# A hybrid two-layer model on one core: state-space chunks spread over two heads, a shared phasor table, and the rotation of the scanned states on GpSimd

## What is computed

```python
proj = hn @ w_in                       # 512 state-space inputs u, then q, k, v, g of 6 retention heads of 256
# state space: 32 groups of 16 channels, 64 complex states each = 16 columns of 128 states
dt = exp(log_dt); mag = exp(lam_re * dt); th = lam_im * dt
ab = mag * (cos(th) + i sin(th)); f = (ab - 1) / lam     # discretisation
bu = u @ (f * b)
x[t] = ab * x[t-1] + bu[t]             # associative scan over the 256 tokens
y = gelu(Re(c x) + d u); y_s5 = y * sigmoid(y @ glu_w + glu_b)
# retention: per head rope(q), rope(k), (q k^T * decay) v, rms norm, times silu(g)
h = h + concat(y_s5, y_ret) @ w_out    # then a gated conv feed-forward, then an attention layer and another one
```

## Time and profile before

| | |
|---|---|
| median of 3 runs | 2261.57 us (2256.18 to 2261.68) |
| profiled execution | 2257.0 us, its span 2255.2 us |
| PE (TensorE matmul) busy | 2162.7 us, 96% |
| DVE (VectorE) busy | 1471.7 us, 65% |
| ACT (ScalarE) busy | 1003.2 us, 44% |
| POOL (GpSimd) busy | 776.3 us, 34% |

### The profile page before, as it was taken

How to read it: one execution, slowest core, us unless ns; L and a number is a source line. 1 busy time by engine, 2 the same in 40 slices (tenths; PEclk the granted TensorE clock), 3 DMA queues, 4 the chain that set the end, 5 groups by cost and what they waited for, 6 DMA issues and landing times.

```text
span 2255.2 us, 47390 instructions
## 1 busy us (share of the span) xinstructions
PE 2162.7 (96%) x18426; PEld 2132.9 (95%) x18426; DVE 1471.7 (65%) x1747; ACT 1003.2 (44%) x1244; POOL 776.3 (34%) x880
## 2 busy tenths in 40 slices
PE   8788888999999999999999999999999999999997
PEld 8788777999999999999999989999999999999997
DVE  6378766577666655666666666677666555666666
ACT  4243333444444444444444445545444444444442
POOL 5799995023434300433411000023443101443311
PEclk9899998999999999999999999999999999999999
DMA  6334233454555456555455533455554556554553
GB/s 262 114 135 154 98 135 125 158 201 178 207 200 187 166 193 221 196 194 186 176 187 198 192 125 123 162 192 188 206 187 174 186 193 220 197 187 185 174 197 114
DMA packets 64604, 398.69 MB, mean 177 GB/s; under 512 B 7169, under 2 KB 9729, under 8 KB 29057
## 3 DMA queue, kind: packets, MB, share of 16 engines
q1 hardware_dynamic: 60192, 391.15, 48.2%
q10 hardware_dynamic: 4320, 6.27, 0.8%
HBM read 395.29 MB, written 2.10 MB: 176 GB/s over the span
## 4 chain that ended last, share of the span: by engine, by line
PE 81%; POOLq 9%; POOL 5%; issue 2%; DVE 2%; ACT 1%; DVEq 0%; DMA 0%; ACTq 0%
PE PS L1401 25%; PE PS L1402 25%; PE PS L1405 25%; POOLq L1288 2%; POOLq L1292 2%; POOL g L1290 2%; POOL E L1293 2%; POOLq L1159 2%; POOLq L1166 1%; PE PS L1396 1%; PE PS L1397 1%; PE PS L1398 1%; POOLq L1306 1%; POOL S L1305 1%; PE PS L1751 0%
## 5 line engine op out<-in xcount | busy, mean ns | idle before, releaser
L705 DVE TENSOR_TENSOR lo<-raw,hi 128x1024 fp32r<-128x1024 f32 (+2 forms) x826 | 950.4, 1170 | 527.0 <-ACT hi L356 521.8
L356 ACT ACTIVATE hi<-raw 128x1024 fp32r<-128x1024 f32 (+2 forms) x826 | 785.8, 969 | 722.2 <-PE PS L1405 676.1
L1401 PE MATMUL PS<-XS,hi 128*128 128x256 f32 x3584 | 851.6, 280 | 8.2 <-ACT hi L356 8.2
L1402 PE MATMUL PS<-XS,hi 128*128 128x256 f32 x3584 | 845.4, 278 | 0.0
L1401 PEld LDWEIGHTS PS<-XS,hi 128*128 128x128 f32 x3584 | 680.2, 190 | 15.8 <-issue 15.4
L1402 PEld LDWEIGHTS PS<-XS,hi 128*128 128x128 f32 x3584 | 680.4, 190 | 0.4
L1405 PE MATMUL PS<-XS,lo 128*128 128x256 f32 x3584 | 480.8, 277 | 0.0
L1405 PEld LDWEIGHTS PS<-XS,lo 128*128 128x128 f32 x3584 | 441.5, 188 | 0.0
L1401 PE MATMUL PS<-YF,hi 128*128 128x256 f32 x1408 | 331.8, 276 | 0.0
L1402 PE MATMUL PS<-YF,hi 128*128 128x256 f32 x1408 | 331.8, 276 | 0.0
L1358 POOL TENSOR_TENSOR ctmp<-apad,cws 128x512 f32<-128x512 f32 x88 | 131.9, 1519 | 526.0 <-DVE apad L756 526.0
(11 more groups left out here) (238 smaller groups left out, 2487.7 us busy)
## 6 DMA issues: line engine op xcount, KB each, us to landing
raw<-in_ffn_up SPq DMA_DIRECT2D x176, 1024.0 KB, 4.8
raw<-in_ffn_dn SPq DMA_DIRECT2D x128, 704.0 KB, 4.1
raw<-in_w_in SPq DMA_DIRECT2D x51, 1024.0 KB, 4.9
raw<-in_w_oe SPq DMA_DIRECT2D x16, 1024.0 KB, 4.8
raw<-in_w_oo SPq DMA_DIRECT2D x16, 1024.0 KB, 4.8
raw<-in_mla_dn SPq DMA_DIRECT2D x9, 1024.0 KB, 4.8
raw<-in_w_ukv SPq DMA_DIRECT2D x8, 1024.0 KB, 4.8
raw<-in_w_uq SPq DMA_DIRECT2D x8, 768.0 KB, 4.3
```

What stands on the lines that cost most here:

```text
L356: act.activation(hi[:, p % SLOTS, 0:n], raw[:, u % SLOTS, off:off + n], ACT.Copy).then_inc(hi_ready, 1)
L705: V.tensor_tensor(lo[:, p % SLOTS, 0:n], raw[:, u % SLOTS, off:off + n], f(hi[:, p % SLOTS, 0:n]), ALU.subtract).then_inc(lo_ready, 1)
L1401: mm(PS[:, bank, 0:T], wh, x[:, 0:T], start=first, stop=False)
L1402: mm(PS[:, bank, 0:T], wh, x[:, T:2 * T], start=False, stop=False)
```

## The change

It has five parts. (1) The levels n = 1 to 16 of all 16 columns are made once (`first_phasors`, the table `E32` in the tile `sums`), and a chunk's `phasors` copies 32 phasors from it and does levels 5 to 7. (2) The rotation forwards moves from VectorE to GpSimd (`rotate_out`), behind a new semaphore `scanned`. (3) The work of a chunk is spread: its second scan comes behind the split of the next head's second K piece, its second C product behind the third K piece of the next head, its B products at other pieces. (4) The end of a head (scaling of G, norm, gate, low half) stands between the splits of the next head instead of behind its own. (5) The set-up is divided: GpSimd computes the exponentials and the powers, VectorE the sine, cosine, factor and B in four parts between the splits of head 0; the transposes of B stand behind the V pieces of head 0 instead of the third G piece; the last sums of squares come earlier, and the first two columns of `U` are scaled ahead of two splits.

GpSimd, and the programs of the chunk:

```diff
+            def double(e, n, lo_, cos_, sin_):
+
+                pool.drain()
+                c_, s_ = lo_
+                G.tensor_tensor(c_, e[:, :, :, 0:n], cos_, ALU.mult)
+                G.tensor_tensor(s_, e[:, :, :, 0:n], sin_, ALU.mult)
+                pool.drain()
+                G.tensor_tensor(e[:, 0, :, n:2 * n], c_[:, 0], s_[:, 1], ALU.subtract)
+                G.tensor_tensor(e[:, 1, :, n:2 * n], c_[:, 1], s_[:, 0], ALU.add)
...
+            def first_phasors():
+
+                G.memset(E32[:, 0, :, 0:1], 1.0)
+                G.memset(E32[:, 1, :, 0:1], 0.0)
+                for l in range(5):
+                    n = 1 << l
+                    c, s_ = (ph[:, l, ri, :].unsqueeze(1).unsqueeze(3).broadcast_to([P, 2, KD, n]) for ri in range(2))
+                    double(E32, n, (g1m[:, :, :, 0:n], g2m[:, :, :, 0:n]), c, s_)
+                pool.drain()
 
             def phasors(k, h0, r):
 
                 m = 4 * h0 + 2 * k
-                G.tensor_copy(phst[:, :, :, :], ph[:, :, :, m:m + 2] if r is None else ph[:, :, :, ds(r * 4 + m, 2)])
                 e = E[:, k]
-                G.memset(e[:, 0, :, 0:1], 1.0)
-                G.memset(e[:, 1, :, 0:1], 0.0)
-                for l in range(8):
+                pool.drain()
+                G.tensor_copy(phst[:, :, :, :], ph[:, 5:8, :, m:m + 2] if r is None else ph[:, 5:8, :, ds(r * 4 + m, 2)])
+                G.tensor_copy(e[:, :, :, 0:32], E32[:, :, m:m + 2, :] if r is None else E32[:, :, ds(r * 4 + m, 2), :])
+                for l in range(5, 8):
                     n = 1 << l
-                    pool.drain()
-                    c, s_ = (phst[:, l, ri, :].unsqueeze(1).unsqueeze(3).broadcast_to([P, 2, 2, n]) for ri in range(2))
-                    G.tensor_tensor(g1[:, :, :, 0:n], e[:, :, :, 0:n], c, ALU.mult)
-                    G.tensor_tensor(g2[:, :, :, 0:n], e[:, :, :, 0:n], s_, ALU.mult)
-                    pool.drain()
-                    G.tensor_tensor(e[:, 0, :, n:2 * n], g1[:, 0, :, 0:n], g2[:, 1, :, 0:n], ALU.subtract)
-                    G.tensor_tensor(e[:, 1, :, n:2 * n], g1[:, 1, :, 0:n], g2[:, 0, :, 0:n], ALU.add)
+                    c, s_ = (phst[:, l - 5, ri, :].unsqueeze(1).unsqueeze(3).broadcast_to([P, 2, 2, n]) for ri in range(2))
+                    double(e, n, (g1[:, :, :, 0:n], g2[:, :, :, 0:n]), c, s_)
...
+            def rotate_out(k, h0, r):
+
+                pool.wait_ge(scanned, at(2 * h0 + k + 1, 2, r))
+                e = E[:, k]
+                G.tensor_tensor(sT2, sT1, e[:, 0:1].broadcast_to([P, 2, 2, T]), ALU.mult)
+                G.tensor_tensor(sB, sT1, e[:, 1:2].broadcast_to([P, 2, 2, T]), ALU.mult)
+                pool.drain()
+                G.tensor_tensor(sT1[:, 0], sT2[:, 0], sB[:, 1], ALU.subtract)
+                G.tensor_tensor(sT1[:, 1], sT2[:, 1], sB[:, 0], ALU.add).then_inc(z_ready, 1)
...
+            def s5_chunk(h0, r):
+
+                if h0:
+                    stage(h0, r)
                 phasors(0, h0, r)
-                pool.drain()
+                rotate_in(0, h0, r)
                 pool.wait_ge(cst_in, at(16 * h0 + 16, 16, r))
                 G.tensor_tensor(Cst[:, :, 1, :], Cst[:, :, 1, :], minus[:, 0:1].unsqueeze(2).broadcast_to([P, 4, 32]),
                                 ALU.mult).then_inc(cneg_ready, 1)
-                rotate_in(0, h0, r)
                 phasors(1, h0, r)
+                rotate_out(0, h0, r)
                 rotate_in(1, h0, r)
+                rotate_out(1, h0, r)
 
             G.memset(minus[:, :], -1.0)
             pool.wait_ge(small_in, 16)
-            pool.wait_ge(den_ready, 1)
-            s5_setup()
+            s5_magnitude()
+            s5_powers()
             pool.wait_ge(bank_free, 2)
             pool.wait_ge(bt_ready, 2)
+            stage(0, None)
+            first_phasors()
             s5_chunk(0, None)
             with pool.Fori(0, 3) as r:
                 s5_chunk(1, r)
```

VectorE: the scans, the places of the head's end, and the set-up:

```diff
@@ -833,25 +946,38 @@
                     dve.wait_ge(w_ready, S_(k + 1, 2))
                     for ri in range(2):
                         for m in range(2):
-                            V.tensor_tensor_scan(sT1[:, ri, m, :], magst[:, m:m + 1].broadcast_to([P, T]),
-                                                 sB[:, ri, m, :], 0.0, ALU.mult, ALU.add)
-                    dve.drain()
-                    eb = E[:, k]
-                    V.tensor_tensor(sT2, sT1, eb[:, 0:1].broadcast_to([P, 2, 2, T]), ALU.mult)
-                    V.tensor_tensor(sB, sT1, eb[:, 1:2].broadcast_to([P, 2, 2, T]), ALU.mult)
-                    dve.drain()
-                    V.tensor_tensor(sT1[:, 0], sT2[:, 0], sB[:, 1], ALU.subtract)
-                    V.tensor_tensor(sT1[:, 1], sT2[:, 1], sB[:, 0], ALU.add).then_inc(z_ready, 1)
-
+                            ins = V.tensor_tensor_scan(sT1[:, ri, m, :], magst[:, m:m + 1].broadcast_to([P, T]),
+                                                       sB[:, ri, m, :], 0.0, ALU.mult, ALU.add)
+                    ins.then_inc(scanned, 1)
...
                 for i in range(4):
-                    if h0 == 0 or i:
-                        split(p0 + 4 + i, 16, r)
+                    if h0 and i == 0:
+                        gate_and_variance(r, h0 - 1)
+                    split(p0 + 4 + i, 16, r)
+                    if h0 == 0:
+                        (s5_angles, s5_phasor, s5_factor, s5_b)[i]()
+                    if h0 and i == 0:
+                        norm_head(r, h0 - 1)
+                    if h0 and i == 1:
+                        head_output(r, h0 - 1)
+                if h0 > 1:
+                    y5()
+                if h0:
+                    y_low(r, h0 - 1)
                 rotate(KRo, p0 + 4, e0)
 
                 for i in range(4):
                     split(p0 + 8 + i, 16, r)
-                    if s5 and i == 1:
+                    if s5 and i == 0:
                         scan(0)
...
-                if s5:
-                    scan(1)
                 if glu:
                     dve.wait_ge(glu_sig, 1)
                     V.tensor_tensor(sigs, sigs, U[:, :, :], ALU.mult).then_inc(glu_mul, 1)
 
                 for i in range(4):
                     split(p0 + 16 + i, 16, r)
+                    if s5 and i == 1:
+                        scan(1)
                     if glu and i == 1:
...
-                scale_banks(Gr[:, :, :], p0 + 16, e0 + 3, 16, r)
-                dve.wait_ge(osum_done, H_(1, 1))
-                norm_head(H_(1, 1))
-                if not glu:
-                    split(p0 + 20, 16, r)
+
+            def gate_and_variance(r, g):
+
+                scale_banks(Gr[:, :, :], 24 + 16 * g, 5 + 4 * g, 16, r)
+                dve.wait_ge(osum_done, at(g + 1, 1, r))
+                V.tensor_scalar(nwt[:, 0, :], PS[:, 4, 0:T], 1.0 / RD, EPS, ALU.mult, ALU.add).then_inc(ovar_ready, 1)
+
+            def norm_head(r, g):
+
+                dve.wait_ge(osd_ready, at(g + 1, 1, r))
+                newton(ro, sq[:, 0, :])
...
+            def s5_angles():
+
+                th, cs, sn, a, b, c = (col(i) for i in (2, 3, 4, 5, 6, 7))
+                dve.wait_ge(th_ready, 1)
...
@@ -801,8 +914,8 @@
                 if c == 0:
                     lambda_squared()
             root(0)
+            scale_banks(U[:, 0:2, :], 7, 0)
             splits(8, kinds=("std",) * 2)
-            scale_banks(U[:, 0:2, :], 7, 0)
             scale_banks(U[:, 2:4, :], 8, 1)
             splits(10, kinds=("std",) * 2)
             dve.wait_ge(even_loads, 48)
```

ScalarE, in `even_head`:

```diff
                 for i in range(4):
-                    if h0 == 0 or i:
-                        split(p0 + 4 + i, 16, r)
-                    if s5 and i == 1:
-                        bu_copy(0)
+                    split(p0 + 4 + i, 16, r)
+                    if h0 and i == 0:
+                        root_and_gate(r, h0 - 1)
+                    if s5 and i in (1, 2):
+                        bu_copy(i - 1)
+                    if s5 and i == 2:
+                        load_c()
+                    if glu and i == 2:
+                        act.wait_ge(c_done, 8)
+                        act.dma_start(gluw, A["gluw"]).then_inc(gluw_in, 16)
+                if h0:
+                    round_y(r, h0 - 1)
...
-                for i in range(4):
-                    split(p0 + 8 + i, 16, r)
-                    if s5 and i == 0:
-                        bu_copy(1)
-
+                splits(p0 + 8, 16, r)
                 for i in range(4):
                     split(p0 + 12 + i, 16, r)
-                    if s5 and i < 2:
-                        bu_copy(i + 2)
+                    if s5 and i in (1, 2):
+                        bu_copy(i + 1)
```

TensorE:

```diff
@@ -1462,11 +1560,9 @@
             for p in range(8):
                 if p % 2 == 0:
                     x_split(0)(p // 2)
-                if p == 6:
-                    x_squares(3)
                 std_piece(p, p // 2, pair(p % 2), XSk)
```

(102 more changed lines are left out.)

213 lines of the change are left out of this document (113 added, 100 removed).

## The result

| | before | changed |
|---|---|---|
| median of 4 runs of each | 2260.24 us (2256.18 to 2261.68) | 2282.83 us (2281.31 to 2285.02) |
| profiled execution, its span | 2257.0, 2255.2 us | 2285.02, 2283.2 us |
| granted clock, mean of the span | 0.982 | 0.975 |

The changed kernel is slower: ratio 1.0104, 95% interval 1.0086 to 1.0121, 22.6 us between the medians. Forecast were +15 and 2276, with a range to 2294.

The account below looks back on a forecast made before the run. GpSimd was taken to bound the heads at 68.4 us a turn; the change makes a ring of 43 + 33 = 76 us. 100.2+4P-378.2-11 gives +15: 2272 profiled, 2276 median, range 2250 to 2294.

Parts of the forecast that it names:

- The ring: Chunk loop: GpSimd's turn becomes a ring with hand-overs, two legs of 43 and 33 us, 76 us against 68.4 before.
- 4P-289: Time difference from before in us, P being one chunk-loop turn on GpSimd; P = 76 gives +15, break-even is 72.3.
- z1 to z0: From a chunk's second rotation out to the next chunk's first: all GpSimd, 32.4 us plus 10.6 of collisions, 43 us.
- z0 to z1: From a chunk's first rotation out to its second: chain through four engines, 33 us, with 18.3 of TensorE work.
- The end of the heads: Last chunk: its second C product, behind three K pieces of head 5, waits shortly without half clock; 11 us back.
- Head 0: First head: the 15.3 us wait goes, TensorE stalls 6 us at the first V piece, head 1 begins about 97.6.
- no relief: GpSimd's uncollided turn: table removes small steps, rotation out adds two blocks of 7.4 us; from 43 to about 47 us.
- VectorE loses 2 x 3.7 us and has slack anyway: Chunk loop: moving the rotation out to GpSimd takes 2 x 3.7 us off VectorE, which was not short of time.
- The ring's waits cost nothing: Rival: GpSimd stays the only bound, turn 68.4 us, time 2246; chance 0.19 together with the rival of vanishing collisions.
- Collisions mostly vanish: Rival: collisions go with the small steps, turn 62 to 66 us, 2221 to 2236; 0.19 shared with the no-cost-waits rival.
- An even swap: Rival: turn 70.6 to 74 us, time within 7 us of before; chance of landing within 0.17.
- VectorE too late in head 0: Rival: small set-up steps at 0.4 us when meeting GpSimd's powers add 7 us, 2283 with turn 76; no separate chance.

Follow-up runs that it names:

- kernel 1: The changed kernel with the rotation of the scanned states back on VectorE, everything else as changed; 2236.73 us, ratio to before 0.9909.
- kernel 4: The changed kernel with VectorE's splits in heads 1 to 4 cut to 64 of 1024 columns, same instruction count; 2238.49 us, ratio to before 0.9913.
- kernel 9: The changed kernel with the second scan ahead of the splits of the next head's K pieces; 2283.66 us, ratio to before 1.0108.
- kernel 6: The kernel before plus the shared phasor table and the divided set-up, rotation and chunk order as before; 2220.92 us, ratio to before 0.9837.
- kernel 2: The kernel before plus the shared phasor table alone; 2240.20 us, ratio to before 0.9917.
- kernel 8: kernel 6 with the rotation of the scanned states moved to GpSimd, in the order of before; 2273.08 us, ratio to before 1.0065.
- kernel 3: The kernel before with only the rotation of the scanned states moved to GpSimd; 2312.12 us, ratio to before 1.0238.
- kernel 7: kernel 1 with the first scan and its rotation behind the second split of the V pieces instead of the first; 2232.68 us, ratio to before 0.9885.
- kernel 5: A separate small kernel, not a model variant: VectorE and GpSimd repeat one operation alone or side by side; 184 us in all.

## Why the prediction was right, and where its sizes were off

**The ring.** Right, and shown. Time follows the turn: 4P-289 with the measured 78.6 gives +25.4, the profiled execution is 28.0 slower, the medians 22.6. In kernel 1, in the same order, the formula gives 4 x 66.5 - 289 = -23 and the ratio -21; in kernel 4 -23 and -20; in kernel 9 +25 and +24.

**z1 to z0, forecast 43 us.** It took 44.0. The two phasor blocks took 11.0 and 15.2 us (forecast 11 to 14, so the second is above). Kernel 4 splits the leg: 8.5 of its 44.0 us are the splits of VectorE. Uncollided 32.4 were forecast; by that estimate 11.6 were lost to VectorE, forecast 10.6. The forecast counted ten splits in this leg, the timeline has nine, so its share of 0.65 was low by more than the leg shows.

**z0 to z1, forecast 33 us.** It took 34.7; this is the larger miss. Up to the output product 19.6 us against 18.3: the half clock was put at 2.6 us of loss, half of some 5 us, but it held from 222.89 to 230.3, 7.4 us, which loses 3.7 (in the kernel before, behind the shorter wait of 6.77 us at 378.19, it held for 5.4). The scan ended at 247.25, 24.5 us behind z0, forecast 23.2, the same shift. The rotation then took 10.2 us, forecast 9.8. GpSimd waited 10.6 for the fourth copy (forecast 6 to 9, so above) and 5.3 for the scan (3 to 6), TensorE 14.2 at each C product (12 to 18).

**The sum.** P was 78.6 instead of 76: 10 us in four turns. The end of the heads returned 9 us instead of 11: 37.2 us of delay at the last C product, 28.0 at the end. So between the profiled executions the miss is 13 us, 28.0 against 15. Between the medians it is 22.6 against 15, a miss of 8; that it is 5 us smaller there is luck: the profiled execution of before lay 3.2 us under its median (the forecast had taken 4.6), that of the changed kernel 2.2 above its own. The mechanism was right; the term sized too small is the turn, 2.6 us short, 1.7 of it in the chain from z0 to z1.

**Head 0.** Right nearly to the row: the wait at the first V piece was 5.6 us (forecast 6), behind it the piece began at 68.2 with its low half (forecast 67.7), head 1 at 97.3 (97.6), `Bst` of chunk 0 at 85.1 (85.6). Kernel 6 against kernel 2 prices the divided set-up at 18 us won (0.9917 less 0.9837, by 2260).

**The parts.** By the same ratios: the table 19 us won, the set-up 18 us won, the interleaving 16 us lost (kernel 6 to kernel 1), the rotation on GpSimd 44 us lost (kernel 1 to the changed kernel). The sum is +23.5, the result, as it must be for steps that lead from one kernel to the other; each step is uncertain by some 5 us and depends on the order. By kernel 8 the rotation costs 52 us (kernel 6 to kernel 8) and the interleaving 9 (kernel 8 to the changed kernel). The prediction had seen that a turn of GpSimd is not shortened (two more blocks of rotation for forty small steps, 47 us against 43 uncollided), but not how much the small steps alone were worth. It called them "no relief" together with the rotation; apart, one wins 19 us and the other loses 54 (kernel 3). It also called VectorE slack: "VectorE loses 2 x 3.7 us and has slack anyway". That is so in the changed kernel; with the rotation on VectorE, in the changed order, VectorE is what TensorE waits for (kernels 1 and 7). Outside head 0 these waits are 34.4 us in kernel 1, against 13.3 for the rotation in kernel 6. This is where most of the 16 us of the interleaving seem to lie; no kernel took it away, and kernel 7 won only 5 of them.

**The rivals.** "The ring's waits cost nothing" fell: GpSimd waits 16 us a turn and the turn is 78.6. "Collisions mostly vanish" fell in the changed kernel; kernel 4 made them vanish by hand and got P = 66.6, just above that rival's 62 to 66. "An even swap" fell with P = 78.6, and "VectorE too late in head 0" with the wait of 5.6 us there.

**Open.** Kernel 8 lies 7 us above what its turn gives: four turns of 6.4 us over before, less the 18 of the set-up, make +8, and it is +15. From `Bst` of chunk 0 to that of chunk 1 it takes 85.3 us against a turn of 74.8, kernel 6 64.2 against 62.3; the shared table is made in that stretch, with GpSimd the bound in one kernel and not in the other. The last C product of kernel 8 begins at 395.43 us, 17.2 later than before, so the surplus has arisen ahead of it and not at the end of the heads. That the table's stretch is the whole reason was not tried. Nor is it excluded that an interleaving with other places for the scans beats kernel 6; only two places were tried.

## What to carry to other kernels

Work moved from VectorE to GpSimd is not fully moved off VectorE while both read two SBUF operands: it is 2.0 times as long (2.30 us for 1.15) and holds up its neighbour, here 44 to 54 us lost in all for 7.4 us of VectorE in each of four chunks. Before moving it, find in the timeline who the turn waits for; what had to go was the many small steps on GpSimd, which beside VectorE's large ones take as long as those. And when a ring of hand-overs has a wait in it, shortening the wait helps only if the place that the work moves to is free: count what stands beside it there.

## What the runs showed of the hardware that was not expected

- The turns are strict, by instruction: 3.3 us a pair for 2.3 and 1.15 alone. The Trainium skill (SBUF — State Buffer, on the engine side's shared port pair) calls it an exclusive lock held for the whole instruction, the other side fully blocked; the runs agree. The forecast had taken shares of 0.65 and 0.75 of VectorE's time. Kernel 4 gives more for the splits: 8.5 us less in the first leg, where 15/16 of nine splits of 1.14 us (9.6 us) were left out.
- A scan over an SBUF tile takes turns as well (2.35 us in place of 0.66); so does a step with one SBUF operand and a constant (2.84 us in place of 0.68); a reciprocal of VectorE costs GpSimd nothing.
- A small step of GpSimd beside large ones of VectorE takes as long as one of those: 1.14 us for 128x16 in kernel 5, 1.18 for 128x2, where it takes 0.20 with little beside it. It costs VectorE nothing that can be seen. Taking forty of them out of a chunk shortened the turn from 68.4 to 62.2 us, where by its busy time TensorE was nearly full.
- The granted clock fell to its lower level of 1.2 GHz after TensorE had waited 14.3 us and stayed there for 7.4 us of work; it did so in each of the four chunks, for 7.3 to 7.9 us.
